# K and V by sections of the features, between the shift and scale tiles, in an adaLN block on one Trainium2 core

## Reference

```python
mod = silu(c) @ w_ada + b_ada            # 2048 x 12288: sh1, sc1, g1, sh2, sc2, g2
mod_c = silu(c_ctx) @ w_ada + b_ada      # of it sh1 and sc1 are used
h  = rmsnorm(x, norm1_g) * (1 + sc1) + sh1
hc = rmsnorm(ctx, norm1_g) * (1 + csc1) + csh1
p = h @ w_in                             # Q 2048, K 512, V 512, Fourier 1024, gates 4096 columns
k, v from p; kc, vc = hc @ w_in[:, K and V columns]
o = attention(q, [k, kc], [v, vc]);  f = fourier_mix(...)
x = x + g1 * ((sig(g_a) * (o @ w_attn_o) + sig(g_f) * (f @ w_fourier)) @ w_out)
x = x + g2 * (relu(h2 @ w1)**2 @ w2);  out = rmsnorm(x, final_norm_g)
```

## Time and profile before

| | |
|---|---|
| median of 3 runs | 1578.26 us (1577.74 to 1579.47) |
| profiled execution | span 1576.3 us from first to last instruction; the page has no other time for it |
| mean granted clock of TensorE | 0.989 |
| PE busy | 1516.4 us, 96% |
| weight loads of PE | 1206.8 us, 77% |
| DVE busy | 927.7 us, 59% |
| ACT busy | 671.7 us, 43% |
| moved | 357.61 MB, mean 227 GB/s |

### The profile page before, as it was taken

One profiled execution on the slowest core, in us unless ns is written; L12 is line 12 of the kernel. 1 busy time (PEld: TensorE's weight loads), 2 busy tenths in 40 slices (PEclk: granted clock), 3 DMA queues, 4 the chain that ended last, 5 costly groups with the idle time before them and its releaser, 6 DMA issues.

```text
span 1576.3 us, 19377 instructions
## 1 busy us (share of the span) xinstructions
PE 1516.4 (96%) x7009; PEld 1206.8 (77%) x7009; DVE 927.7 (59%) x1042; ACT 671.7 (43%) x931; POOL 25.4 (2%) x38
## 2 busy tenths in 40 slices
PE   4989999999999999999998999999999999999996
PEld 1446888878788887877876888888888888888885
DVE  1336665777676668776877554444445455555456
ACT  2324243645544444333345434444434444444443
POOL 0000100101000000000000000000000000000001
PEclk8999999999999999999999999999999999999998
DMA  9999587776676668968883666556555555555551
GB/s 339 321 333 323 198 308 230 257 251 204 203 239 216 210 230 323 315 230 314 319 296 111 195 195 190 183 183 185 167 190 178 207 193 192 194 190 196 189 200 77
DMA packets 108234, 357.61 MB, mean 227 GB/s; under 512 B 11024, under 2 KB 12048, under 8 KB 107024
## 3 DMA queue, kind: packets, MB, share of 16 engines
q1 hardware_dynamic: 105984, 351.32, 65.2%
q10 hardware_dynamic: 2192, 5.51, 0.9%
HBM read 354.68 MB, written 2.10 MB: 226 GB/s over the span
## 4 chain that ended last, share of the span: by engine, by line
PE 87%; DMA 5%; DVE 4%; ACT 2%; issue 1%; POOL 1%; ACTq 0%; SPq 0%; DVEq 0%; POOLq 0%
PE bank L1211 26%; PE bank L1213 26%; PE bank L1212 26%; DMA raw<-in_w_ada 3%; PE bank L1348 2%; PE bank L1330 2%; PE bank L1374 1%; PE bank L1450 1%; DVE wl L909 1%; PE bank L1338 1%; ACT wh L585 1%; DMA raw<-in_w_out 1%; PE bank L1243 1%; DMA raw<-in_w_fourier 1%; DVE acc L929 1%
## 5 line engine op out<-in xcount | busy, mean ns | idle before, releaser
L909 DVE TENSOR_TENSOR wl<-raw,wh 128x1024 fp32r<-128x1024 f32 x464 | 564.0, 1224 | 505.8 <-ACT wh L585 504.8
L585 ACT ACTIVATE wh<-raw 128x1024 fp32r<-128x1024 f32 x464 | 486.1, 1059 | 461.9 <-PE bank L1213 441.4
L1211 PE MATMUL bank<-wh,hT 128*128 128x512 f32 x512 | 209.1, 408 | 3.6 <-DVE wl L909 1.7
L1211 PE MATMUL bank<-wh,h2T 128*128 128x512 f32 x512 | 202.8, 396 | 2.4 <-DVE h2T L1097 2.4
L1213 PE MATMUL bank<-wh,hT 128*128 128x512 f32 x512 | 201.0, 393 | 0.0
L1212 PE MATMUL bank<-wl,hT 128*128 128x512 f32 x512 | 200.2, 391 | 0.0
L1213 PE MATMUL bank<-wh,h2T 128*128 128x512 f32 x512 | 200.0, 391 | 0.0
L1212 PE MATMUL bank<-wl,h2T 128*128 128x512 f32 x512 | 199.6, 390 | 0.0
L1211 PE MATMUL bank<-wh,hidS 128*128 128x512 f32 x512 | 199.5, 390 | 0.0
L1213 PE MATMUL bank<-wh,hidS 128*128 128x512 f32 x512 | 199.4, 390 | 0.0
L1212 PE MATMUL bank<-wl,hidS 128*128 128x512 f32 x512 | 199.4, 389 | 0.0
(11 more groups left out here) (168 smaller groups left out, 1498.9 us busy)
## 6 DMA issues: line engine op xcount, KB each, us to landing
raw<-in_w SPq DMA_DIRECT2D x256, 512.0 KB, 3.6
raw<-in_w_ada SPq DMA_DIRECT2D x192, 512.0 KB, 5.6
raw<-in_w_in SPq DMA_DIRECT2D x128, 512.0 KB, 4.6
raw<-in_w_attn_o SPq DMA_DIRECT2D x32, 512.0 KB, 5.6
raw<-in_w_out SPq DMA_DIRECT2D x32, 512.0 KB, 6.0
raw<-in_w_fourier SPq DMA_DIRECT2D x16, 512.0 KB, 6.0
xt<-in_x ACTq DMA_DIRECT2D x2, 1024.0 KB, 8.6
ct<-in_ctx ACTq DMA_DIRECT2D x2, 1024.0 KB, 14.1
```

The lines of the kernel that those rows point to most:

```text
L585: nc.scalar.activation(slot, raw[:, s % RAW, :], ACT.Copy).then_inc(wh_done, 1)
L909: nc.vector.tensor_tensor(lo, raw[:, s % RAW, :], hi.bitcast(F32), ALU.subtract)\
L1211: nc.tensor.matmul(bank[b][:], a_hi, w_hi, start=first, stop=False)
```

## The change

The 16 feature blocks are cut into six sections of 2, 2, 4, 4, 2 and 2 blocks. S and C tiles are of one section (a 2-block section has tiles of four row blocks by 256 columns, 4 tiles a name). K and V of section s become chunks of their own (K0, V0, ..., K5, V5; 1, 1, 2, 2, 1, 1 tiles), placed between the S and C tiles of section s + 1; K5 and V5 stand behind the last C tile. MODS then end at position 77 (before: 69); F starts at position 80 in both kernels. Each K or V chunk is evacuated by DVE, two positions after its last tile: a copy for section 0, an add into SBUF for the others. The tokens are loaded by SP ahead of the weights, their squares and scaling stand at positions 0 to 3, all transposes at positions 5 to 11, K's transposes at F + 10. SP no longer waits for the constant vectors. The ratio of the ADA multiply-adds is 0.68.

From the lists, with post(m - 2) written at its place: DVE has at 35 the split of V1 and the additions of C2, at 36 modulate 2, at 37 the adds of V1, at 39 modulate 3, at 40 the split of K2's first tile; at 77 the split of V4, the additions of C5 and modulate 7, at 78 the split of K5, at 79 the split of V5, two multiply-adds and the adds of V4, at 80 the split of F's first tile, one multiply-add and the adds of K5.

```diff
-CHUNKS = [("K", 8), ("V", 8), ("F", 16), ("Q0", 16), ("Q1", 16), ("GA0", 16), ("GA1", 16),
+SECTIONS = [(0, 2), (2, 2), (4, 4), (8, 4), (12, 2), (14, 2)]
+NS = len(SECTIONS)
+CHUNKS = [(kind + str(s), n // 2) for s, (_, n) in enumerate(SECTIONS) for kind in "KV"]
+KV = [name for name, _ in CHUNKS]
+SECTION = {f"{kind}{s}": section for s, section in enumerate(SECTIONS) for kind in "SCKV"}
+LAST_K, LAST_V = f"K{NS - 1}", f"V{NS - 1}"
+CHUNKS += [("F", 16), ("Q0", 16), ("Q1", 16), ("GA0", 16), ("GA1", 16),
...
-MODS = [kind + str(q) for q in range(4) for kind in "SC"]
-TWO_BLOCKS = ["K", "V"] + MODS
+MODS = [kind + str(s) for s in range(NS) for kind in "SC"]
+P_LAST = len(MODS) - 1
 MOD_BANK = {"S": 4, "C": 7}
-K_AMONG = {("S1", 6), ("C1", 2), ("S2", 6), ("C2", 2), ("S3", 6)}
-K_LEAD = 3
-TILES, _k = [], 0
-for _name in MODS:
-    for _n in range(KT // 2):
-        TILES.append((_name, _n))
-        if (_name, _n) in K_AMONG:
-            TILES.append(("K", _k))
-            _k += 1
-MODS_END = len(TILES)
+FETCH_LEAD = 3
+def mod_tiles(name):
+    return KT * SECTION[name][1] // 8
+def front():
+    tiles = []
+    for s, (_, n) in enumerate(SECTIONS):
+        mods = [(kind + str(s), i) for kind in "SC" for i in range(mod_tiles(f"S{s}"))]
+        behind = [(kind + str(s - 1), i) for kind in "KV" for i in range(SECTIONS[s - 1][1] // 2)] if s else []
+        for i, tile in enumerate(mods):
+            tiles.append(tile)
+            while behind and (i + 1) * (SECTIONS[s - 1][1]) >= len(mods) * (SECTIONS[s - 1][1] - len(behind) + 1):
+                tiles.append(behind.pop(0))
+    return tiles
+TILES = front()
+MODS_END = 1 + max(m for m, (name, _) in enumerate(TILES) if name in MODS)
 for _name, _n in CHUNKS:
-    TILES += [(_name, k) for k in range(_k if _name == "K" else 0, _n)]
+    if (_name, 0) not in TILES:
+        TILES += [(_name, k) for k in range(_n)]
...
-FETCH = [m for m, (name, _) in enumerate(TILES[:MODS_END]) if name in MODS]
+FETCH = []
 for _m, (_name, _n) in enumerate(TILES):
-    if _name == "K" and _m <= MODS_END:
-        FETCH.insert(_m - K_LEAD, _m)
-    elif _m >= MODS_END:
+    if _name in KV and _m <= MODS_END:
+        FETCH.insert(len(FETCH) - FETCH_LEAD, _m)
+    else:
         FETCH.append(_m)
...
-    _units += 0.0 if _m < MODS_END + 2 else 2.0 if _name in "KV" else 1.0
+    _units += 0.0 if _m < MODS_END + 2 else 2.0 if _name in KV else 1.0
     ADA_AT[_m] = []
-    while _n < 128 and _n < _units * 0.62:
+    while _n < 128 and _n < _units * 0.68:
...
-K_TILES = dict(CHUNKS)["K"]
-K_AT = [TILES.index(("K", k)) for k in range(K_TILES)]
-MODULATE = {K_AT[k] - 2: k for k in range(5)} | {K_AT[k]: k for k in (5, 6, 7)}
-X_IN = {n: n for n in range(4)}
-SQX = {4 + 2 * n: n for n in range(4)}
-XN = {11 + n: n for n in range(4)}
-TAB_K = 44
-MOD_COLS = {LAST[name] + (3 if name != MODS[-1] else 0): p for p, name in enumerate(MODS)}
-MOD_ADD = {LAST[name] + 5: p for p, name in enumerate(MODS[:-1])}
-XTR = {14 + 2 * n: (("x", "c")[n % 2], n // 2) for n in range(16)}
+SQX = {n: n for n in range(4)}
+XN = {n: n for n in range(4)}
+TAB_LOAD, TAB_K = FIRST["S3"], FIRST["S4"]
+def c_columns(s):
+    return LAST[f"C{s}"] if s in (0, NS - 1) else FIRST[f"S{s + 1}"] - 1
+MOD_COLS = {LAST[f"S{s}"] + 3: 2 * s for s in range(NS)} | {c_columns(s): 2 * s + 1 for s in range(NS)}
+MOD_ADD = {LAST[f"S{s}"] + 3: 2 * s for s in range(NS)} | {c_columns(s): 2 * s + 1 for s in range(NS - 1)}
+MOD_ADD[MODS_END] = P_LAST
+MODULATE = {(MODS_END if s == NS - 1 else c_columns(s) + (2 if s == 0 else 1) + 3 * i): f0 // 2 + i
+            for s, (f0, n) in enumerate(SECTIONS) for i in range(n // 2)}
+SECTION_OF = {f0 // 2 + i: s for s, (f0, n) in enumerate(SECTIONS) for i in range(n // 2)}
+XTR = {5: (0, 1), 8: (2, 3), 9: (4, 5), 10: (6,), 11: (7,)}
+XTR = {m: [(src, n) for n in keys for src in "xc"] for m, keys in XTR.items()}
 FOUR1 = {FIRST["Q0"] + 1 + d: d for d in range(8)}
 FOUR2 = {FIRST["Q0"] + 9 + g: g for g in range(4)}
 FOUR_LO = {FIRST["Q0"] + 10 + g: g for g in range(4)}
-KTR = {FIRST["V"] + 6 + t: t for t in range(4)}
+KTR = {FIRST["F"] + 10 + t: t for t in range(4)}
...
+            for n in range(4):
+                t, source = ((xt, x), (ct, ctx_))[n // 2]
+                sp.dma_start(t[:, n % 2, :], source[n % 2 * P:(n % 2 + 1) * P, :]).then_inc(tokens_in[n], 16)
...
-                if s == 3:
-                    sp.wait_ge(vec_in, 96)
...
-                if m == LAST["K"]:
...
-                    evacuate("K", ACT.Copy, lambda b: kraw[:, b, :])
...
-                    evacuate("V", ACT.Copy, lambda b: v[:, b, :])
...
+                if TILES[m][0] in KV and m == LAST[TILES[m][0]]:
+                    name = TILES[m][0]
+                    ci = CI[name]
+                    if ci < 2:
+                        misc_wait_freed(dve, ("xc"[ci], 7))
+                    for b in range(4):
+                        part = {"K": kraw, "V": v}[name[0]][:, b, :]
+                        wait_bank(dve, ci, m, b)
+                        if ci < 2:
+                            nc.vector.tensor_copy(part, bank[b][:]).then_inc(bank_free, 1)
+                        else:
+                            dve.wait_ge(bank_free, 4 * (ci - 2) + b + 1)
+                            nc.vector.tensor_tensor(part, part, bank[b][:], ALU.add).then_inc(bank_free, 1)
...
-                if name == "K":
-                    pe.wait_ge(h_lo, 2 * (k + 1))
+                if name in KV and name[0] == "K":
+                    pe.wait_ge(h_lo, SECTION[name][0] + 2 * k + 2)
...
+                    blocks, w = 8 // SECTION[name][1], SECTION[name][1] * P
+                    for j in range(blocks):
+                        kk = blocks * k + j
                         rows_k = slice(kk % GROUPS * P // GROUPS, (kk % GROUPS + 1) * P // GROUPS)
-                        ins = nc.tensor.matmul(bank[MOD_BANK[name[0]]][rows_k, :], cc32[:, kk, :],
-                                               raw[:, s % RAW, j * HC:(j + 1) * HC],
+                        ins = nc.tensor.matmul(bank[MOD_BANK[name[0]]][rows_k, 0:w], cc32[:, kk, :],
+                                               raw[:, s % RAW, j * w:(j + 1) * w],
...
+                        if k == 0 and CI[name]:
+                            pe.wait_ge(bank_free, 4 * CI[name] - 3 + t)
```

More of the change, by code:

```diff
@@ L171 @@
     if _m in XTR:
-        MISC.append(XTR[_m])
+        MISC += XTR[_m]
     if _m in ADA_SUM:
@@ L445, in tile_source @@
                 r = slice(k * P, (k + 1) * P)
[L446 to L450, removed]
+                if name in SECTION:
+                    f0, n = SECTION[name]
+                    w, col = {"K": (w_in, K0), "V": (w_in, V0), "S": (w_ada, f0 * P), "C": (w_ada, D + f0 * P)}[name[0]]
+                    row0, t, width = (f0 + 2 * k, 2, HC) if name in KV else (8 // n * k, 8 // n, n * P)
+                    return w[row0 * P:(row0 + t) * P, col:col + width].rearrange("(t p) n -> p t n", p=P)
                 col0 = {"F": FO0, "Q0": 0, "Q1": NC, "GA0": GA0, "GA1": GA0 + NC, "GF0": GF0, "GF1": GF0 + NC}
@@ L479, in _ @@
                 dst = raw[:, s % RAW, :]
-                if kind == "M" and TILES[a][0] in TWO_BLOCKS:
-                    dst = dst.rearrange("p (t n) -> p t n", t=2)
+                if kind == "M" and TILES[a][0] in SECTION:
+                    dst = dst.rearrange("p (t n) -> p t n", t=2 if TILES[a][0] in KV else 8 // SECTION[TILES[a][0]][1])
                 sp.dma_start(dst, src).then_inc(raw_full[s % RAW], 16)
@@ L636, in post @@
                         misc_wait_full(act, ("mod", p - 2))
-                    nc.scalar.activation(modrow[:, p % 2, :], bank[MOD_BANK[name[0]]][:], ACT.Copy)\
+                    w = SECTION[name][1] * P
+                    nc.scalar.activation(modrow[:, p % 2, 0:w], bank[MOD_BANK[name[0]]][:, 0:w], ACT.Copy)\
                         .then_inc(modrow_ready, 1)
-                if m in XTR:
-                    key = XTR[m]
+                for key in XTR.get(m, []):
                     b = misc_wait_full(act, key)
@@ L869, in mod_columns @@
             def mod_columns(p):
-                quarter, kind = divmod(p, 2)
+                section, kind = divmod(p, 2)
+                f0, n = SECTIONS[section]
                 b = misc_wait_full(dve, ("mod", p))
-                f = slice(4 * quarter, 4 * quarter + 4)
-                bias = cols[:, 64 + 16 * kind + 4 * quarter:68 + 16 * kind + 4 * quarter]
-                mine = b[:, 0:8].rearrange("p (f v) -> p f v", v=2)
+                f = slice(f0, f0 + n)
+                bias = cols[:, 64 + 16 * kind + f0:64 + 16 * kind + f0 + n]
+                mine = b[:, 0:2 * n].rearrange("p (f v) -> p f v", v=2)
                 for vv in range(2):
@@ L889, in modulate @@
             def modulate(k):
-                dve.wait_ge(gain_ready, k // 2 + 1)
+                dve.wait_ge(gain_ready, SECTION_OF[k] + 1)
                 if k:
@@ L1251, in hook @@
```

(21 more changed lines are left out.)

27 lines of the change are left out of this document (9 added, 18 removed).

## The result

The changed kernel takes 1615.49 us, median of 4 runs (1609.42 to 1617.9), against 1578.00 for the kernel before beside it: 1.0236 times as long, 95% interval 1.0215 to 1.0257. The forecast was 1609 us in a range of 1574 to 1624. The profiled execution is the quickest of the four: 1609.42 us, span 1607.6.

What follows compares the result with a forecast made beforehand. The prediction took a front end of about 130 us, then PE's own work, to bound the kernel. Terms 21.7 + 4.7 + 0.7 + 3.4 = 30.5 on the 1576.3 us span gave a 1609 us median forecast, range 1574 to 1624.

Steps and rivals of the forecast that it cites:

- The main step: From K0 to F, PE waits for DVE's chain in program order; F starts at 214.5 against 192.84 us, +21.7.
- K0's start: Front end: the first K tile begins near 44.5 us, 7.7 earlier than before, bounds 41 and 48.
- The gaps 82: Between K and V tiles up to F: 82 us, of which 35 PE's own small work and 47 waits.
- The handovers: In the gaps between K and V tiles: 0.2 us priced for each handover between engines.
- The clock term: Tiles behind new waits: two falls of PE's clock to half, +3.4 us, bounds 0 and 13.6.
- The row I let decide: Profile rows of 72 to 104 us: clock at 1.00 with one DMA wait of 7.6 us, taken to speak for fewer falls.
- +4.7 for DVE's load: F's start to its eighth tile: DVE has 24.0 us of work against PE's 19.1; +4.7, bounds 0 and 7.
- The transposes: At F: two transposes of K that ran before F come after it, +0.7 us.
- The first: Rival, gaps between K and V tiles: waits are hidden, F at 167.5, end at 1558 us; chance 0.12.
- The second: Rival, same gaps: 24 of 47 us of waits go, F at 191, end at 1585 us; chance 0.18.
- The third: Rival, K and V tiles: the clock falls at every wait, 13.6 in place of 3.4, 1620 us; chance 0.12.
- DMA would be late next: Front end: without DVE's chain, DMA would be the next to be late, at 118 us for the last modulation tile.

Runs made afterwards that it cites:

- experiment 7: Changed kernel with extra fp32 products of constants on PE in idle time ahead of K1 to K4 and V1 to V3: 1607.44 us, ratio 1.0184.
- Experiment 6: Changed kernel with adds and splits earlier, one modulate step later, and Q's rotation tables six positions later: 1583.63 us, ratio 1.0035 to the kernel before.
- experiments 1 and 5: Changed kernel with adds at the chunk's own last position, 1593.02 us; the same with splits three positions early and one modulate step later, 1586.40 us.
- experiment 3: Changed kernel with only the second modulate step of section 2 moved from ahead of K2's first tile to behind it: 1612.92 us, ratio 1.0228.
- experiment 9: Kernel before with tokens loaded first and the splits of K tiles among the modulation tiles three positions early: 1571.60 us, ratio 0.9963.

## Why the prediction was right, step by step

**The main step held.** F's start was forecast 21.7 us later and came 26.2 later, 10.5 of it clock, which the sum has in a term of its own; without it 15.7. PE waits for DVE in the gaps. The single-change runs tell the cause apart: moving the adds, the splits or one modulate step shortens just the gaps whose chain holds them, doubling the adds lengthens them, and DMA's ring was seen to limit one gap, K1 to V1, when the chain is cut.

**Its terms**, forecast and measured, from K0 to F: K0's start 44.5, came 46.9 (the constant vectors arrived at 13.05, not 12, and four groups of transposes ran at half clock, 1.1 us and not 0.66). The gaps 82, came 73.5: K to V of a 2-block section 5.6, 6.6 and 5.7 for 6.4, of a 4-block one 6.1 and 5.7 for 6.9, V to K 7.7 to 8.3 for 8.6 to 9.1, V1 to K2 11.3 for 12.1, V4 to K5 1.7 beyond V4's slowed tile (3.3 beyond a full-speed one, as forecast). The handovers were counted twice in part, since DVE's pieces overlap by some 0.06 us each: the four adds take 2.47, not 2.75, though one is 0.68, as in the row I took the earlier trace rows.

**The clock term was mis-sized.** I took two falls, 3.4 us. The front end has seven stretches at half clock between 38 us and F, six tiles are 1.4 to 2.2 us longer, 10.5 in all, and F's eighth tile adds 2.4; 12.9 against the bound of 13.6. The row I let decide, 1.00 across a wait of 7.6 us, was misread. From 72 to 104 us PE has no such wait; its longest idle time is 2.0 us, within sparse small work:

```profile
79.90 1.05 PE L1374 MATMUL bank<-raw,cc 128*32 128x512 f32 x4 [2.04 <-DMA raw<-in_w_ada]
```

So nothing spoke for a clock that stays up across waits like those of the change, and the half-clock rows ahead of K5 were the better pattern. The Trainium skill ("TensorE: Matmul & The Clock Gate", HAM oscillation) tells of a product whose waits for data throttle the engine again at every K tile. The trace agrees in part. The four tiles behind the longest idle times of PE (4.0 to 8.5 us, ahead of K2, K3, V3 and K4) fell, to 0.70 to 0.79, and so did two behind shorter ones (V2, 3.0 us, and V4, 1.9). But V0, K1 and V1, with 3.0, 1.5 and no more than 1.2 us, ran at 1.00:

```profile
58.10:63.70 5.60, 5.56 (x24) 4.59 (x25) 0.00 (x0) 0.00 (x0) 0.00 (x0) 1.00 0.83 273
71.50:77.10 5.60, 5.55 (x24) 4.42 (x24) 0.00 (x0) 0.00 (x0) 0.00 (x0) 1.00 1.05 385
83.60:89.20 5.60, 5.60 (x26) 4.61 (x25) 0.00 (x0) 0.60 (x1) 0.00 (x0) 1.00 1.03 374
```

In experiment 7, where the waits were filled, the six slow tiles ran at 1.00, V4 too, whose own wait was not filled; V0 and K5 fell instead. The gaps' surplus (8.5) and the clock's deficit (9.5) nearly cancel, which is why the profiled span, 1607.6, is so close to the 1606.8 of the sum; that closeness is luck.

**F.** +4.7 for DVE's load (24.0 less 19.1 is 4.9) came as 3.6 of wait ahead of F's eighth tile, the tile that was named. Experiment 6 takes 1.7 us of DVE's work away and the wait falls by 1.7, as the cause given demands. The transposes came as 1.0 for 0.7. Nothing was counted for the waits for g1row (2.1 less), for the other waits for split weights (1.6 more) and for the two falls of the clock that only the kernel before has behind F (3.3 less).

**The rivals.** The first (waits hidden, F at 167.5) is excluded by F at 219. The second (24 of the 47 us of waits go) is excluded by the gaps: they lost 8.5 us of the forecast 82. The third (the clock falls at every wait, 1620) was nearly true, with six of nine tiles slowed and 12.9 for its 13.6, and should have had a larger chance than 0.12: the measured median, 1615.5, lies nearer to its time than to the 1609 of the forecast. That DMA would be late next if the chain were gone was said in one sentence, and is what experiments 1 and 5 met.

**Open.** The median lies 6 us above the profiled execution, and the three other runs of the changed kernel have a mean clock of 0.978 to 0.982 in place of 0.985. Worked out from these shares, their clock lacks 5 to 11 us more than the profiled one's (an estimate), and their spans are 5.6 to 8.5 us longer. So more falls of the clock would explain it, and traces do differ in them behind F (one stretch at half clock in the changed kernel, three in that of experiment 3), but there is no trace of those runs. The medians of the changed kernel and of experiment 7 are 8.1 us apart, their profiled spans 1.7; that isn't explained either. What each half of experiment 9 is worth is open too.

DMA was costed at nothing, and no experiment tests one part of that: tiles of 256 columns. The page counts 28432 packets under 2 KB in place of 12048, and in the stretch that has these tiles the changed kernel moves 275 GB/s at a share of 0.86, the kernel before with tokens first 387 at 1.05:

```profile
15.00:45.00 30.00, 21.47 (x150) 11.13 (x151) 8.55 (x16) 16.27 (x25) 1.22 (x2) 0.94 0.86 275
```

```profile
15.00:45.00 30.00, 26.34 (x113) 6.54 (x114) 8.07 (x16) 11.30 (x15) 1.22 (x2) 1.00 1.05 387
```

That is 320 for 369 GB/s of a full share (an estimate). It did not bind the gaps of the changed kernel, where PE waits 1.9 us for w_ada; what it costs ahead of K0, or once the orders are mended, isn't shown.

## What to carry to other kernels

An engine that is 44% busy can bind another that is 79% busy (DVE and PE from 44 to 219 us), if both run their work in a fixed order and each step starts with a wait for the other: price the chain between two pieces of the bound engine's work, not the busy shares. Work that only needs what is there early (a split, an add of the banks that are full) goes ahead of the first wait in its engine's order. And cutting a product into pieces with waits between them can cost the clock as well as the waits: here 1.4 to 2.2 us a tile, in six tiles of nine.

## What was unexpected of the hardware

Loads of 8 and 16 KB on ACT's queue, issued by 5.1 us, landed at 13.05 us behind 4 MB of tokens on SP's queue, where they had landed at 8.85. The first modulation product did not wait for them, as its weights came at 15.4, but ACT's squares of the tokens, which stand behind them, began at 13.98; a kernel that waits for such vectors would see 4.2 us. Loading the 4 MB first, which delays the first modulation product by 4.8 us, still made the kernel before 4.5 us faster.
